# The softmax probabilities of the one-map attentions are scaled by VectorE in place of GpSimd

## The chip, the cores and the metric

The kernel runs on one core of a Trainium2 chip. The metric is the device time of one execution in microseconds (us); the median of several executions counts. The engines are named as in the profile: PE is TensorE's matmul and PEld its weight load, DVE is VectorE, ACT is ScalarE, POOL is GpSimd, SP is SyncE, which issues the DMAs.

## The reference, cut to what matters

A sequence of 512 tokens with 1024 features passes two blocks of two layers each, all in float32. Three of the attentions have one softmax map per head:

- attention A, in both layers of the first block: 8 heads of 64, causal, keys selected by an index score;
- MLA attention, in both layers of the second block: 4 heads, queries and keys of 96, all 512 keys;
- cross attention, in both layers of the second block: 4 heads of 64 on 256 memory rows.

```python
def one_block(qblk):
    sc = jnp.einsum('bqhd,bkhd->bhqk', qblk, k).astype(jnp.float32) * scale
    p = jax.nn.softmax(sc, axis=-1)
    return jnp.einsum('bhqk,bkhe->bqhe', p.astype(v.dtype), v)
```

A fourth, attention B of the first block, subtracts two softmax maps (`a1 - lam * a2`). The change does not touch it.

## The kernel before, in words

All engine programs are written out by hand, with semaphores between engines, and each stage ends in a barrier of all engines. Weights stream in as tiles of 128x1024: SyncE loads a tile into `raw` (a ring of 2, `Weights.load`, L341), ScalarE copies its rounded high part (`split_high`, L350), GpSimd subtracts it for the low part (`split_low`, L359), and TensorE makes three passes per product with high and low parts (`product`, L373 to L375). `split_low` of a tile waits for the tile's high part.

`attention_work` (L674) writes the four engine programs of an attention. Its unit `n` is one block of 128 queries of one head; units go in pairs over two heads, so the query block `i` is `(n % 8) // 2`. `width(i)` is the number of keys: 128, 256, 384, 512 in the causal attention A, always 512 in MLA attention, 256 in cross attention. For a unit:

- TensorE computes the scores into a bank (`scores`, L698);
- VectorE takes the row maximum: L793 with the selection bias in attention A, L796 in the others, which then negate and scale it (L799 in MLA attention, L801 in cross attention);
- ScalarE takes the exponential with its row sum (L760);
- VectorE takes the reciprocal of the sum (L809), one step later;
- GpSimd multiplies the exponentials by it into `prob(n)` (L834), one of 2 buffers in attention A and one of 4 in the others (`depth`); it waits for the reciprocal, and for the transposes of unit `n - depth`;
- TensorE transposes the block (`turn`, L707), `lag` steps after the scores (2 in attention A, 4 in the others);
- ScalarE copies the transposed block to `PT` (L769);
- TensorE multiplies by the values after each 8 units (`value`, L713), and ScalarE copies the result out (L778).

TensorE takes two units at a time: scores, scores, turn, turn. Other work of the stage is laid between the steps by `side_pe`, `side_act`, `side_dve` and `side_pool`. In attention A these are seven tiles of gate products, half a tile per pair of units (`gate_half`), each followed by a multiplication on VectorE that empties the bank (`gate_scale`, L1209; the next gate product waits for it), the splits of their weight tiles, and the normalization of attention B's output at the start. In MLA attention it is the preparation of the memory in eight chunks: ScalarE's scaled copy and square (L503, L509), VectorE's low part and sum (L513, L520), one chunk per step. In cross attention there is none. There GpSimd's program is all splits up to the attention, then the attention, then all splits behind it.

For a map count of 2 (attention B) GpSimd scales the second map (L829) and VectorE combines both (L817); that stays.

Of the kernel before, what the change touches and what calls it, by code (L numbers as in the profile page):

```python
# [18 lines left out]
ALU = mybir.AluOpType  # L19
# [552 lines left out]
def build(nc, x_in, w1, small1, const_in, p_in, w2, small2, masks_in, mem_in, pos_in, out):  # L572
    sem = Semaphores(nc)

    def sb(name, shape, dt=F32):
        return nc.alloc_sbuf_tensor(name, shape, dt)
# [14 lines left out]
    tmp = sb("tmp", [P, 10, SEQ])  # L591
# [11 lines left out]
    stat = sb("stat", [P, 4, 32])  # L603
# [70 lines left out]
    def attention_work(heads, maps, scale, q, k, width, bias, v, m_out, out_of, n_blocks, causal, neg_lambda=None, side_act=None, side_dve=None,  # L674
# [3 lines left out]
        E, LOGIT = 0, 4  # L678
        lag, PROB = (2, (8, 9)) if bias else (4, (4, 5, 6, 7))
        depth = len(PROB)  # L680

        def prob(n):

            return tmp[:, PROB[n % depth], 0:width(unit(n)[1])]

        def unit(n):

            two, r = divmod(n, 2 * NT)
            return 2 * two + r % 2, r // 2
# [92 lines left out]
        def run_dve(dve):  # L782
            for step in range(N + 1):
                if step < N:
                    n = step
                    h, i = unit(n)
                    for m in range(maps):
                        s = n * maps + m
                        dve.wait_ge(sem("scored"), s + 1)
                        if bias:  # L790
                            if s >= 4:
                                dve.wait_ge(sem("exp_done"), s - 3)
                            dve.tensor_tensor_reduce(tmp[:, LOGIT + s % 4, 0:width(i)], banks[s % 4][:, 0:width(i)], bias(i),  # L793
                                                     1.0, -2 * MASKED, ALU.add, ALU.min, stat[:, 0, s:s + 1]).then_inc(sem("max_ready"), 1)
                            continue
                        dve.tensor_reduce(stat[:, 0, s:s + 1], banks[s % 4][:, 0:width(i)], AX.X, ALU.max).then_inc(sem("max_ready"), 1)  # L796
                        dve.wait_ge(sem("max_ready"), s + 1)
                        if query_col:
                            dve.tensor_scalar(stat[:, 1, s:s + 1], stat[:, 0, s:s + 1], query_col(h, i), -1.0, ALU.mult, ALU.mult).then_inc(sem("neg_ready"), 1)  # L799
                        else:  # L800
                            dve.tensor_scalar(stat[:, 1, s:s + 1], stat[:, 0, s:s + 1], -scale, None, ALU.mult).then_inc(sem("neg_ready"), 1)  # L801
                if side_dve:
                    side_dve(dve, step, "scores")
                n = step - 1
                if 0 <= n:
                    h, i = unit(n)
                    s = n * maps
                    dve.wait_ge(sem("exp_done"), s + maps)
                    dve.reciprocal(stat[:, 3, s:s + maps], stat[:, 2, s:s + maps]).then_inc(sem("rsum_ready"), 1)  # L809
                    if maps == 2:  # L810
                        dve.wait_ge(sem("rsum_ready"), n + 1)
                        dve.tensor_scalar(stat[:, 3, s + 1:s + 2], stat[:, 3, s + 1:s + 2], neg_lambda, None,
                                          ALU.mult).then_inc(sem("lambda_ready"), 1)
                        dve.wait_ge(sem("second_scaled"), n + 1)
                        if n >= depth:
                            dve.wait_ge(sem("transposed"), n - depth + 1)
                        dve.scalar_tensor_tensor(prob(n), tmp[:, E + s % 4, 0:width(i)], stat[:, 3, s:s + 1],  # L817
                                                 tmp[:, E + (s + 1) % 4, 0:width(i)], ALU.mult, ALU.add).then_inc(sem("prob_ready"), 1)
                if side_dve:
                    side_dve(dve, step, "end")  # L820

        def run_pool(pool):
            for n in range(N):
                h, i = unit(n)
                s = n * maps
                if maps == 2:
                    e2 = tmp[:, E + (s + 1) % 4, 0:width(i)]
                    pool.wait_ge(sem("lambda_ready"), n + 1)
                    pool.tensor_scalar(e2, e2, stat[:, 3, s + 1:s + 2], 1.0, ALU.mult, ALU.mult).then_inc(sem("second_scaled"), 1)  # L829
                else:  # L830
                    pool.wait_ge(sem("rsum_ready"), n + 1)
                    if n >= depth:
                        pool.wait_ge(sem("transposed"), n - depth + 1)
                    pool.tensor_scalar(prob(n), tmp[:, E + s % 4, 0:width(i)], stat[:, 3, s:s + 1], 1.0,  # L834
                                       ALU.mult, ALU.mult).then_inc(sem("prob_ready"), 1)
                if side_pool:
                    side_pool(pool, n)
        return run_pe, run_act, run_dve, run_pool

    def attention(weights, prefetch, work, before=None):  # L840
# [1845 lines left out]
```

## Time and profile before

| | |
|---|---|
| median of 3 runs | 3483.81 us (3483.07 to 3484.43) |
| profiled execution | 3483.18 us |
| its span | 3481.4 us |
| PE busy | 3182.5 us (91%) |
| DVE busy | 1670.7 us (48%) |
| ACT busy | 1435.2 us (41%) |
| POOL busy | 1576.3 us (45%) |
| POOL, L359 (low parts) | 482 of 2430 ns |
| POOL, L834 (probabilities) | 128 of 562 ns |
| attention A, first layer | 294.6 to 384 us of the span |
| MLA attention, first layer | 2072.8 to 2121.9 us |
| cross attention, first layer | 2229.7 to 2254 us |
| PE busy in attention A, first layer | 80.25 of 89.4 us |

The shares of busy time are averages over stages that differ. For a change inside three of them the stages have to be read apart. Each attention stands twice in the program, once per layer.

### The profile page before, as it was taken

How to read it: one execution, taken by the hardware profiler on the slowest of the kernel's cores; microseconds unless marked ns; L12 is line 12 of the kernel's file. 1: busy time of each engine (PE TensorE's matmuls, PEld its weight loads, DVE VectorE, ACT ScalarE, POOL GpSimd, SP SyncE). 2: the span in 40 equal slices, each digit the busy share in tenths (PEclk: the TensorE clock that was granted, in tenths of full speed). 3: DMA queues.
4: the chain of work that ended last, by engine and by line, in shares of the span. 5: the costliest groups of instructions: out<-in, count | busy, mean ns of one | idle time of the engine just before them, and what ended most of it. 6: DMA issues, size and time to landing. Idle time of an engine off the chain costs nothing. (4 is left out here: it accounts for less than half of the span.)

```text
span 3481.4 us, 39157 instructions
## 1 busy us (share of the span) xinstructions
PE 3182.5 (91%) x14620; PEld 2474.4 (71%) x14620; DVE 1670.7 (48%) x2524; ACT 1435.2 (41%) x2281; POOL 1576.3 (45%) x870
## 2 busy tenths in 40 slices
PE   7978899999998799999999967899999985979999
PEld 6655688878766567887878735578887852758877
DVE  2773347731357533775235883433313785443320
ACT  4736533333384554333343454432223355352221
POOL 4623545544563354554456332334445432234443
PEclk8989999999899999999999978999999997989999
DMA  3111233323211112332322101223333200213333
GB/s 112 61 55 43 69 95 97 97 91 103 76 61 61 37 55 91 103 97 94 103 86 89 52 12 37 66 81 97 96 103 98 67 25 27 65 49 97 97 97 103
DMA packets 73740, 265.09 MB, mean 76 GB/s; under 512 B 8656, under 2 KB 9168, under 8 KB 73168
## 3 DMA queue, kind: packets, MB, share of 16 engines
q1 hardware_dynamic: 73552, 262.59, 24.1%
q8 instruction: 117, 1.92, 0.2%
q14 instruction: 71, 0.58, 0.1%
HBM read 260.46 MB, written 2.10 MB: 75 GB/s over the span
## 5 line engine op out<-in xcount | busy, mean ns | idle before, releaser
L359 POOL TENSOR_TENSOR low<-raw,high 128x1024 fp32r<-128x1024 f32 x482 | 1170.7, 2430 | 1298.8 <-ACT high L350 1276.0
L374 PE MATMUL bank<-slot_r,low 128*128 128x512 f32 (+2 forms) x3636 | 1434.6, 395 | 0.0
L375 PE MATMUL bank<-slot_r,high 128*128 128x512 f32 (+2 forms) x3636 | 1432.1, 394 | 0.0
L373 PE MATMUL bank<-slot_r,high 128*128 128x512 f32 (+1 forms) x3316 | 1339.9, 404 | 100.0 <-POOL low L359 22.5
L350 ACT ACTIVATE high<-raw 128x1024 fp32r<-128x1024 f32 x482 | 507.3, 1054 | 848.2 <-PE bank L375 819.1
L373 PEld LDWEIGHTS bank<-slot_r,high 128*128 128x128 f32 x3316 | 636.5, 192 | 286.5 <-issue 69.4
L374 PEld LDWEIGHTS bank<-slot_r,low 128*128 128x128 f32 (+1 forms) x3636 | 696.4, 192 | 148.9 <-issue 9.2
L375 PEld LDWEIGHTS bank<-slot_r,high 128*128 128x128 f32 (+1 forms) x3636 | 695.4, 191 | 149.8
L1568 DVE SCALAR_TENSOR_TENSOR tmp<-padded,small,tmp 128x512 f32<-128x512 f32 x176 | 209.9, 1251 | 0.0
L834 POOL TENSOR_SCALAR tmp<-tmp,stat 128x512 f32<-128x512 f32 (+3 forms) x128 | 72.0, 562 | 195.4 <-DVE stat L809 167.1
L698 PE MATMUL bank<-slots 64*128 64x256 f32 (+4 forms) x384 | 96.1, 509 | 44.5 <-PEq L320 40.7
L503 ACT ACTIVATE slot_r<-slots,small 128x512 fp32r<-128x512 f32 (+1 forms) x80 | 54.7, 684 | 196.6 <-DVE slots L1547 61.1
L2615 DVE TENSOR_TENSOR tmp<-bank,rs 128x512 f32<-128x512 f32 x44 | 30.4, 692 | 207.3 <-PE bank L375 196.3
L707 PE MATMUL bank<-const,tmp 128*128 128x128 f32 x432 | 74.8, 292 | 59.9 <-ACT PT L769 25.9
L1559 DVE TENSOR_TENSOR padded<-bank,rs 128x512 f32<-128x512 f32 x88 | 60.4, 686 | 138.7 <-PE bank L375 126.5
L2048 DVE SCALAR_TENSOR_TENSOR slots<-padded,small,slots 128x512 f32<-128x512 f32 x128 | 122.0, 1009 | 0.0
L707 PEld LDWEIGHTS bank<-const,tmp 128*128 128x128 f32 x432 | 52.6, 147 | 91.8 <-issue 39.4
L2509 ACT ACTIVATE tmp<-tmp 128x512 f32<-128x512 f32 x44 | 27.8, 633 | 211.6 <-DVE tmp L2615 211.6
L769 ACT ACTIVATE PT<-bank 128x256 f32<-128x256 f32 (+3 forms) x160 | 72.1, 456 | 98.8 <-PE bank L713 51.9
L2625 DVE TENSOR_TENSOR tmp<-bank,rs 128x512 f32<-128x512 f32 x16 | 11.1, 691 | 210.8 <-PE bank L375 210.8
L760 ACT ACTIVATE tmp<-tmp,stat 128x128 f32<-128x128 f32 (+3 forms) x128 | 71.0, 555 | 97.6 <-DVE stat L793 97.0
L1576 DVE TENSOR_TENSOR slots<-slots,bank 128x512 f32<-128x512 f32 x16 | 11.0, 687 | 197.0 <-PE bank L375 197.0
(310 smaller groups left out, 3661.6 us busy)
## 6 DMA issues: line engine op xcount, KB each, us to landing
raw<-w SPq DMA_DIRECT2D x482, 512.0 KB, 3.5
slots<-x_in SPq DMA_DIRECT2D x4, 512.0 KB, 6.6
slots<-mem_in SPq DMA_DIRECT2D x2, 1024.0 KB, 4.9
out<-slots SPq DMA_DIRECT2D x8, 256.0 KB, 4.8
const<-const_in SPq DMA_DIRECT2D x1, 1073.5 KB, 10.6
padded<-p_in SPq DMA_DIRECT2D x2, 512.0 KB, 5.5
tmp<-masks_in SPq DMA_DIRECT2D x1, 512.0 KB, 11.4
small<-small SPq DMA_DIRECT2D x2, 231.5 KB, 2.7
```

The costliest lines, as they stand in the source:

```text
L350: act.activation(self.high[:, t % PARTS, :], self.raw[:, t % RING, :], ACT.Copy).then_inc(self.sem("tile_high"), 1)
L359: pool.tensor_tensor(self.low[:, t % PARTS, :], self.raw[:, t % RING, :], self.high[:, t % PARTS, :].bitcast(F32), ALU.subtract).then_inc( ...
L373: pe.matmul(acc, lhs[0], rhs[1], start=first, stop=False)
L374: pe.matmul(acc, lhs[1], rhs[0], start=False, stop=False)
L375: return pe.matmul(acc, lhs[0], rhs[0], start=False, stop=last)
L698: pe.matmul(banks[s % 4][:, 0:width(i)], q(h, m, i), k(h, m, width(i)), start=True, stop=True).then_inc(sem("scored"), 1)
L707: mm = pe.transpose(banks[4 + n % 2][:, j * P:j * P + P], prob(n)[:, j * P:j * P + P], cst("ident"))
L760: act.activation(tmp[:, E + s % 4, 0:width(i)], src, ACT.Exp, scale=by, bias=most, accum_out=stat[:, 2, s:s + 1]).then_inc(sem("exp_done"), 1)
L769: act.activation(PT[:, h % 2, 0:b, i * P:i * P + P], banks[4 + n % 2][:, 0:width(i)].rearrange("p (b t) -> p b t", b=b), ACT.Copy).then_in ...
L834: pool.tensor_scalar(prob(n), tmp[:, E + s % 4, 0:width(i)], stat[:, 3, s:s + 1], 1.0, ALU.mult, ALU.mult).then_inc(sem("prob_ready"), 1)
L1568: dve.scalar_tensor_tensor(o, padded_t[:, s % 4, 15 - tap:15 - tap + SEQ], s1("conv_w", (2 - tap) * 2 * FC + ch), o, ALU.mult, ALU.add).th ...
L2048: ins = dve.scalar_tensor_tensor(o, src, s2(w, 2 * j + c), o, ALU.mult, ALU.add)
```

## The change

The branch for one map moves from GpSimd's program to the end of VectorE's step. VectorE waits for its own reciprocal and for the buffer, multiplies, and signals `prob_ready`. Nothing else is altered. Lines behind the added ones are shifted: in the changed kernel the new multiplication is L823, and the gate multiplication L1209 is L1208.

```diff
@@ run_dve, after the reciprocal of unit n
                         dve.scalar_tensor_tensor(prob(n), tmp[:, E + s % 4, 0:width(i)], stat[:, 3, s:s + 1],
                                                  tmp[:, E + (s + 1) % 4, 0:width(i)], ALU.mult, ALU.add).then_inc(sem("prob_ready"), 1)
+                    else:
+                        dve.wait_ge(sem("rsum_ready"), n + 1)
+                        if n >= depth:
+                            dve.wait_ge(sem("transposed"), n - depth + 1)
+                        dve.tensor_scalar(prob(n), tmp[:, E + s % 4, 0:width(i)], stat[:, 3, s:s + 1], None, ALU.mult).then_inc(sem("prob_ready"), 1)
                 if side_dve:
                     side_dve(dve, step, "end")
@@ run_pool
                     pool.wait_ge(sem("lambda_ready"), n + 1)
                     pool.tensor_scalar(e2, e2, stat[:, 3, s + 1:s + 2], 1.0, ALU.mult, ALU.mult).then_inc(sem("second_scaled"), 1)
-                else:
-                    pool.wait_ge(sem("rsum_ready"), n + 1)
-                    if n >= depth:
-                        pool.wait_ge(sem("transposed"), n - depth + 1)
-                    pool.tensor_scalar(prob(n), tmp[:, E + s % 4, 0:width(i)], stat[:, 3, s:s + 1], 1.0,
-                                       ALU.mult, ALU.mult).then_inc(sem("prob_ready"), 1)
                 if side_pool:
                     side_pool(pool, n)
```

GpSimd's queue in attention A, first layer, from unit 14 to unit 31, before (L834 is a probability, L359 a low part):

```order
L834 TENSOR_SCALAR tmp<-tmp,stat 128x512 x2
L359 TENSOR_TENSOR low<-raw,high 128x1024
L834 TENSOR_SCALAR tmp<-tmp,stat 128x128 x2
L834 TENSOR_SCALAR tmp<-tmp,stat 128x256 x2
L359 TENSOR_TENSOR low<-raw,high 128x1024
L834 TENSOR_SCALAR tmp<-tmp,stat 128x384 x2
L834 TENSOR_SCALAR tmp<-tmp,stat 128x512 x2
L359 TENSOR_TENSOR low<-raw,high 128x1024
```

The same queue in the changed kernel, for the whole stage (L1303 is a low part of attention B's output):

```order
L1303 TENSOR_TENSOR slot_r<-slots,slot_r 128x512
L359 TENSOR_TENSOR low<-raw,high 128x1024 x2
L1303 TENSOR_TENSOR slot_r<-slots,slot_r 128x512 x2
L359 TENSOR_TENSOR low<-raw,high 128x1024
L1303 TENSOR_TENSOR slot_r<-slots,slot_r 128x512
L359 TENSOR_TENSOR low<-raw,high 128x1024 x5
```

The probabilities that stood between two low parts are gone, and with them their waits.

VectorE's queue in MLA attention, first layer, one step with memory work and the next step's first rows, before:

```order
L809 RECIPROCAL stat<-stat 128x1
L796 TENSOR_REDUCE stat<-bank 128x1
L799 TENSOR_SCALAR stat<-stat,col 128x1
L513 SCALAR_TENSOR_TENSOR slot_r<-slots,small,slot_r 128x256
L520 TENSOR_TENSOR slots<-slots 128x256
L809 RECIPROCAL stat<-stat 128x1
```

And in the changed kernel:

```order
L809 RECIPROCAL stat<-stat 128x1
L823 TENSOR_SCALAR tmp<-tmp,stat 128x512
L796 TENSOR_REDUCE stat<-bank 128x1
L799 TENSOR_SCALAR stat<-stat,col 128x1
L513 SCALAR_TENSOR_TENSOR slot_r<-slots,small,slot_r 128x256
L520 TENSOR_TENSOR slots<-slots 128x256
L809 RECIPROCAL stat<-stat 128x1
```

The multiplication stands between a reciprocal and the next unit's reduction.

VectorE's queue in attention A, first layer, around the gate multiplication of units 15 to 17, before and, behind it, in the changed kernel:

```order
L793 ISA tmp,stat<-bank,selbias 128x128
L793 ISA stat 128x1
L809 RECIPROCAL stat<-stat 128x1
L1209 TENSOR_TENSOR slots<-bank,rs 128x512
```

```order
L793 ISA tmp,stat<-bank,selbias 128x128
L793 ISA stat 128x1
L809 RECIPROCAL stat<-stat 128x1
L823 TENSOR_SCALAR tmp<-tmp,stat 128x128
L1208 TENSOR_TENSOR slots<-bank,rs 128x512
```

The probability of the unit before now stands ahead of the gate's multiplication.

## Rows read from the trace of the kernel before

**Rows 1.** Line L834: durations (min/median/max), and who waited for it (us, times)
```profile
L834 POOL TENSOR_SCALAR tmp<-tmp,stat x128: 372/536/704, 296.3 to 3079.5; 128x256 f32<-128x256 f32 x48, 128x512 f32<-128x512 f32 x48, 128x128 f32<-128x128 f32 x16, 128x384 f32<-128x384 f32 x16
...
  PEld bank L707: 28.6, 26
  PE bank L707: 8.0, 6
```

**Rows 2.** Timeline, MLA attention, one step: start us, us, engine, line, operation, idle before
```profile
2086.01 0.78 ACT L760 ACTIVATE tmp<-bank,stat,col 128x512 f32<-128x512 f32 x1
2087.95 0.79 ACT L760 ACTIVATE tmp<-bank,stat,col 128x512 f32<-128x512 f32 x1
...
2086.59 0.15 DVE L809 RECIPROCAL stat<-stat 128x1 f32<-128x1 f32 x1
2086.66 0.67 DVE L796 TENSOR_REDUCE stat<-bank 128x1 f32<-128x512 f32 x1
2087.80 0.48 DVE L513 SCALAR_TENSOR_TENSOR slot_r<-slots,small,slot_r 128x256 fp32r<-128x256 f32 x1 [0.22 <-ACT slot_r L503]
2088.54 0.15 DVE L809 RECIPROCAL stat<-stat 128x1 f32<-128x1 f32 x1
```

**Rows 3.** Timeline, cross attention: first and last of 12 exponentials, one reduction and negation
```profile
2231.18 0.47 ACT L760 ACTIVATE tmp<-bank,stat 128x256 f32<-128x256 f32 x1 [0.19 <-DVE stat L801]
2239.42 0.48 ACT L760 ACTIVATE tmp<-bank,stat 128x256 f32<-128x256 f32 x1
...
2235.20 0.41 DVE L796 TENSOR_REDUCE stat<-bank 128x1 f32<-128x256 f32 x1
2235.64 0.15 DVE L801 TENSOR_SCALAR stat<-stat 128x1 f32<-128x1 f32 x1
```

**Rows 4.** One line, L1146: duration ns min/median/max of its forms
```profile
L1146 DVE TENSOR_SCALAR selbias<-PT,slots x6: 354/421/488, 86.5 to 1016.6; 128x256 f32<-128x256 f32 x2, 128x384 f32<-128x384 f32 x2, 128x512 f32<-128x512 f32 x2
```

**Rows 5.** Timeline, VectorE: a reciprocal and the operation that waits for it
```profile
2960.68 0.18 DVE L2535 RECIPROCAL col<-col 128x4 f32<-128x4 f32 x1 [18.80 <-ACT col L2454]
2960.89 0.29 DVE L2540 TENSOR_SCALAR tmp<-const,col 128x128 f32<-128x128 f32 x1
```

**Rows 6.** Timeline, attention A, first layer: around two gate multiplications
```profile
349.07 1.05 ACT L350 ACTIVATE high<-raw 128x1024 fp32r<-128x1024 f32 x1
350.64 0.16 DVE L809 RECIPROCAL stat<-stat 128x1 f32<-128x1 f32 x1 [0.89 <-ACT tmp L760]
351.35 2.37 POOL L359 TENSOR_TENSOR low<-raw,high 128x1024 fp32r<-128x1024 f32 x1
351.95 0.60 PE L707 MATMUL bank<-const,tmp 128*128 128x128 f32 x4
352.24 0.67 DVE L1209 TENSOR_TENSOR slots<-bank,rs 128x512 f32<-128x512 f32 x1
353.54 0.50 PE L373 MATMUL bank<-slot_r,high 128*128 128x512 f32 x1
...
357.31 1.05 ACT L350 ACTIVATE high<-raw 128x1024 fp32r<-128x1024 f32 x1
359.09 0.16 DVE L809 RECIPROCAL stat<-stat 128x1 f32<-128x1 f32 x1 [1.13 <-ACT tmp L760]
362.04 0.50 PE L373 MATMUL bank<-slot_r,high 128*128 128x512 f32 x1
```

**Rows 7.** Timeline: a low part on GpSimd and two VectorE operations beside it
```profile
2984.46 2.40 POOL L359 TENSOR_TENSOR low<-raw,high 128x1024 fp32r<-128x1024 f32 x1 [7.15 <-ACT high L350]
2984.61 2.52 DVE L2540 TENSOR_SCALAR tmp<-const,col 128x128 f32<-128x128 f32 x2
```

**Rows 8.** Busy time by stretch, MLA attention: value products, and what came before the second
```profile
2098.06:2101.64 3.58, 3.58 (x17) 1.06 (x16) 0.16 (x1) 0.06 (x1) 3.02 (x2) 1.00 0.00 0
2113.05:2119.60 6.55, 6.52 (x16) 1.71 (x16) 0.00 (x0) 0.00 (x0) 0.00 (x0) 0.56 0.00 0
2102.00:2108.60 6.60, 3.32 (x16) 1.72 (x14) 2.04 (x6) 6.55 (x13) 2.41 (x3) 1.00 0.26 79
```

## Prediction

> **What bounds the kernel now.** The change touches 128 multiplications, so I first looked at who waits for them. On GpSimd they take 372 to 704 ns, and TensorE waited for one of them 8.0 us in all and its weight loads 28.6 us [rows 1]. Next I took apart the six stages that hold them, attention A, MLA attention and cross attention, each for two layers. Each stands between barriers or in one engine order, so that what a stage loses the program loses. They have different limits. Attention A is TensorE's once its gate products run: it goes from transposes (351.95) through the next scores to the next gate product (353.54) without a stop [rows 6]. In MLA attention TensorE is light and ScalarE sets the pace: one step is an exponential, its sum, a copy, and a scaled copy and a square of the memory, from 2086.01 to 2087.95 in the same order each time; the exponential to exponential distance is 1.95 us, and VectorE's is the same, reciprocal to reciprocal [rows 2]. What the reader is to see there is VectorE's idle time inside the step: 0.22 us. It is the second engine of that loop, with nearly no room. Cross attention is alike without the memory work: 12 exponentials start from 2231.18 to 2239.42 [rows 3].
>
> **The change part by part.** It removes 128 multiplications from GpSimd and puts one behind each reciprocal on VectorE, with two waits ahead of it (for the reciprocal, and for the transposes that free the buffer).
>
> *Price of one.* The nearest row is L1146: the same operation with one per-row scalar, SBUF to SBUF, 354, 421 and 488 ns for 256, 384 and 512 columns [rows 4]. I take these. The bounds: below, 0.29 us, which L2540 takes for 128 columns [rows 5]; above, the GpSimd times of [rows 1] (0.70 for 512). An operation that reads a reciprocal starts 0.21 us after it (2960.68 to 2960.89) [rows 5], and one that doesn't wait starts some 0.08 before the recorded end of the one ahead: the reciprocal at 2086.59 lasts 0.15, and the reduction starts at 2086.66 [rows 2]. A 512-column scale so holds VectorE 0.41 and a 256-column one 0.28, plus 0.13 of waiting (0.20 from the reciprocal where it was 0.07, [rows 2]): 0.54 and 0.41 us per step. [...]
>
> *MLA attention, per layer.* VectorE's step is 1.95 - 0.22 = 1.73 us of work [rows 2]; with 0.54 it is 2.27, over ScalarE's 1.95. Eight steps carry memory work (the eight chunks), each loses 0.32: 2.6 us until the first value products can start. Behind them the tail is ScalarE's and TensorE's and keeps its length: VectorE has two reductions and four reciprocals left in it and is idle for the most part. Two layers: **+5.2**. Bounds: a scale of 0.29 us makes the step 2.07 and the term +2, one of 0.70 makes it 2.48 and the term +8.5.
>
> *Cross attention, per layer.* Reduction to negation is 0.44 (2235.20 to 2235.64) [rows 3], negation to reciprocal 0.07, reciprocal to scale 0.20, scale 0.28: 0.99 us per step. From the first exponential to the twelfth there are eleven steps; the first has no scale (0.52), ten at 0.99, and 0.2 until the first ends: 10.6 against 8.24 now, +2.4. The products behind wait for the copy after the twelfth. Two layers: **+4.8**; bounds +2 and +8.
>
> *Attention A, per layer.* Here TensorE needs a probability one or two steps later, behind half a tile of gate products, so its own length costs nothing. What costs is GpSimd's other work. The split of a weight tile's low part (L359, 2.37 us) stood behind a probability on GpSimd's queue; now it starts when its high part is done (349.07 + 1.05, so 350.2 in place of 351.35) [rows 6]. The scale on VectorE reads and writes SBUF only, and such an operation does not run beside L359: of two L2540 that started at 2984.61, 0.15 after an L359, both ended only at 2987.13, where the clean ones take 0.29; the L359 ran from 2984.46 to 2986.86 [rows 5, 7]. So the scale of unit 19, due at 350.64 + 0.20 = 350.84, ends at about 352.75. Its transposes were due on TensorE at 352.2: +0.65. Then VectorE still owes the maximum (0.49), the reciprocal, the scale of unit 20 (0.20 + 0.35) and only then the gate's multiplication L1209 (0.67), which the next gate product waits for: 354.6 against 353.54, **+1.07** [rows 6]. Three places per layer look so (L1209 at 333.5, 352.2, 371.5). At the other two (341.4, 360.6) the split runs from 358.45 to 360.8, the 512-column scale due at 359.3 ends at 361.0, and 0.22 + 0.20 + 0.21 + 0.69 + 0.1 later the gate product may start, at 362.4 against 362.04 [rows 6]: +0.4. The last transposes lose 0.2. Sum 3.2 + 0.8 + 0.2 = 4.2, two layers **+8.4**. The stage's first 28 us belong to ScalarE's table loads; there the shorter hand-over gains some tenths and collisions lose some: I take zero, bounds -1 and +1 per layer. The bounds of the term: +0.5 if nothing collides, +11.
>
> *GpSimd itself* is freed of 72 us; nobody waits for its splits in these stages, so this is worth nothing. In cross attention the next tile's split now runs before the attention instead of behind it, and the tile is used after it either way. DMA issues are the same and come earlier.
>
> **Sum:** 8.4 + 5.2 + 4.8 = +18.4 us. The profiled execution took 3483.18 us, 0.6 below the median of the runs, 3483.81; on the median that is 3502.2, and I write 3502.0. A measurement of this kernel tells 0.2% (7 us) from no change.
>
> **The rivals.**
> *No collision.* If the scale gets past L359, attention A loses 0.2 per layer and the sum is 5.2 + 4.8 + 0.4 = 10.4: 3494. For it: only [rows 7] speaks against, and with another first input. 0.16. [...]
>
> *The clock falls.* [...] Against: no row shows a fall during the steps themselves. 0.12.
>
> *The cover holds.* If VectorE's waits in both loops hide most of the scale (the 0.22 of [rows 2] is what this one step shows; early steps and the tail have more), some 3 us are left: 3487. 0.08.
>
> *The shorter chain wins*, slower turned to faster. One hand-over and 0.1 to 0.2 us of duration per probability go: a 512-column one is ready 0.25 us sooner after its reciprocal (0.70 + 0.10 against 0.49 + 0.05). Where TensorE waits for it, 32 times [rows 1], this gives 32 x 0.2 = 6.4 us, and an L359 ending sooner in front of a VectorE operation with two SBUF inputs gives 1 us twice: 3475. It decides if VectorE's loop in MLA has more than 0.54 us of room per step; the row shows 0.22. [...] 0.05.
>
> **How the numbers follow.** The forecast has 0.59. Range 3489 to 3511: it holds the forecast with its bounds, the no-collision case and nearly all of the clock case, and leaves out the last two and the far bounds. Slower by over 0.2% is the forecast, no collision and the clock: 0.87. Within 0.2%: 0.08. Faster: 0.05.
>
> **What would show it.** In MLA attention VectorE's reciprocals 2.2 to 2.3 us apart where they were 1.95, with no idle time left, and ScalarE's exponentials waiting for the negation; the stage 2.6 us longer. In cross attention exponentials 1 us apart and the stage 2.4 longer. In attention A an L359 starting right behind L350, a scale of 1.5 to 2.4 us beside it, TensorE's transposes waiting for VectorE, and the stage 4 us longer. Wrong would be: all scales at 0.3 to 0.5 us beside L359 (no collision); a granted clock of 0.5 in the first value products; or an idle time on VectorE that outlasts the scale.

## Result and profile after

The changed kernel takes 3501.51 us (median of 5 runs, 3500.14 to 3504.93), against 3483.07 for the kernel before in the same measurement: 1.0054 times as long, 95% interval 1.0043 to 1.0065. That is +18.4 us; the prediction was 3502.0. The profiled execution of the change is the slowest of its five, 3504.93 us with a span of 3503.2.

The page after, busy time of each engine, and the line of the multiplication (L823, in place of [rows 1]):

```profile
PE 3196.1 (91%) x14620; PEld 2479.2 (71%) x14620; DVE 1740.9 (50%) x2652; ACT 1439.4 (41%) x2281; POOL 1507.1 (43%) x742
...
L823 DVE TENSOR_SCALAR tmp<-tmp,stat x128: 285/421/1905, 297.6 to 3100.6; 128x256 f32<-128x256 f32 x48, 128x512 f32<-128x512 f32 x48, 128x128 f32<-128x128 f32 x16, 128x384 f32<-128x384 f32 x16
...
  PEld bank L707: 56.1, 54
  PE bank L707: 13.1, 19
```

The median multiplication became shorter (421 ns against 536), the longest one far longer (1905 against 704), and TensorE waits for it 69.2 us in place of 36.6.

**MLA attention** after, timeline of VectorE, one step of the first layer (answers [rows 2]):

```profile
2102.32 0.16 DVE L809 RECIPROCAL stat<-stat 128x1 f32<-128x1 f32 x1
2102.51 0.49 DVE L823 TENSOR_SCALAR tmp<-tmp,stat 128x512 f32<-128x512 f32 x1
2102.91 0.68 DVE L796 TENSOR_REDUCE stat<-bank 128x1 f32<-128x512 f32 x1
2103.63 0.21 DVE L799 TENSOR_SCALAR stat<-stat,col 128x1 f32<-128x1 f32 x1
2103.76 0.48 DVE L513 SCALAR_TENSOR_TENSOR slot_r<-slots,small,slot_r 128x256 fp32r<-128x256 f32 x1
2104.15 0.42 DVE L520 TENSOR_TENSOR slots<-slots 128x256 f32<-128x256 f32 x1
2104.49 0.16 DVE L809 RECIPROCAL stat<-stat 128x1 f32<-128x1 f32 x1
```

No idle time is left, and the step is 2.17 us (1.95 before).

**Attention A** after, timeline of the first layer around a gate multiplication (answers [rows 6]):

```profile
353.19 2.40 POOL L359 TENSOR_TENSOR low<-raw,high 128x1024 fp32r<-128x1024 f32 x1 [9.05 <-ACT high L350]
353.63 0.17 DVE L809 RECIPROCAL stat<-stat 128x1 f32<-128x1 f32 x1 [0.89 <-ACT tmp L760]
353.83 1.91 DVE L823 TENSOR_SCALAR tmp<-tmp,stat 128x256 f32<-128x256 f32 x1
...
355.80 0.44 PE L707 MATMUL bank<-const,tmp 128*128 128x128 f32 x2 [0.44 <-DVE tmp L823]
356.66 0.68 DVE L1208 TENSOR_TENSOR slots<-bank,rs 128x512 f32<-128x512 f32 x1
```

The low part starts right behind its high part (352.06 + 1.05), and a multiplication of 256 columns that begins 0.64 us later lasts 1.91, until the low part is over; alone the same multiplication takes 0.35. Six per layer do this (1.82 to 1.91 us). Two multiplications per layer of MLA attention do it too (1.54 and 1.72 us, behind the steps with memory work). They cost nothing there: the second value products start 15.0 us after the first, as in before.

**Where the time went.** One row is a kernel, one column a stretch, in us: how much more lies between the starts of the same two TensorE instructions than in the profile of before. The last four rows are experiments of the next section.

| | start to 41 | A, layer 1 (294 to 400) | A, layer 2 (1192 to 1300) | other stretches to 2072 | from 2072 to the end | sum |
|---|---|---|---|---|---|---|
| the change | +1.4 | +6.5 | +6.4 | +0.6 | +6.9 | +21.8 |
| A only | -0.8 | +5.1 | +6.5 | +4.4 | +0.2 | +15.4 |
| A only, from the bank | -0.4 | -0.2 | -0.1 | -0.5 | 0.0 | -1.1 |
| A only, short low parts | -0.7 | -0.3 | +1.0 | +2.9 | +2.4 | +5.3 |
| the same again | -0.5 | +0.9 | +1.0 | +5.4 | +2.3 | +9.2 |

The first column lies ahead of every changed instruction and has either sign; it is not the change's. So does the time up to 294 us, with 1.8 of the 4.4 us of A only in the fourth column. The profiles of the change and of A only are the slowest executions of their five, 3.4 and 3.0 us over the median, so their rows add up to more than the medians say.

### The profile page after: what moved, and what is told of

It is laid out like the page before. It is cut to its first block and busy times, and to the rows that moved or that the text cites. A ratio compares the mean times of both kernels' runs of the same rounds, so it can differ in the third digit from the quotient of the medians.

```text
span 3503.2 us, 39157 instructions
## 1 busy us (share of the span) xinstructions
PE 3196.1 (91%) x14620; PEld 2479.2 (71%) x14620; DVE 1740.9 (50%) x2652; ACT 1439.4 (41%) x2281; POOL 1507.1 (43%) x742
## 5 line engine op out<-in xcount | busy, mean ns | idle before, releaser
L359 POOL TENSOR_TENSOR low<-raw,high 128x1024 fp32r<-128x1024 f32 x482 | 1171.9, 2433 | 1509.6 <-ACT high L350 1479.9
L707 PE MATMUL bank<-const,tmp 128*128 128x128 f32 x432 | 84.0, 314 | 65.9 <-ACT PT L769 26.3
L698 PEld LDWEIGHTS bank<-slots 64*128 64x128 f32 (+1 forms) x384 | 42.1, 210 | 86.2 <-issue 80.7
```

The source lines that it names most:

```text
L359: pool.tensor_tensor(self.low[:, t % PARTS, :], self.raw[:, t % RING, :], self.high[:, t % PARTS, :].bitcast(F32), ALU.subtract).then_inc( ...
L698: pe.matmul(banks[s % 4][:, 0:width(i)], q(h, m, i), k(h, m, width(i)), start=True, stop=True).then_inc(sem("scored"), 1)
L707: mm = pe.transpose(banks[4 + n % 2][:, j * P:j * P + P], prob(n)[:, j * P:j * P + P], cst("ident"))
```

## The experiments

All are times of whole kernels beside runs of before, which has a median of 3483.0 to 3483.3 in each measurement.

### One stage at a time

The place of the multiplication becomes a choice of each caller (`on_dve`); each run has one stage on VectorE and the others on GpSimd.

```diff
-                    else:
+                    elif on_dve(n):
                         dve.wait_ge(sem("rsum_ready"), n + 1)
@@ run_pool
+                elif not on_dve(n):
+                    pool.wait_ge(sem("rsum_ready"), n + 1)
...
```

> Only attention A scales on VectorE; MLA and cross attention stay as before. By the traces of before and after, each layer of A lost 4.8 us and TensorE's lower clock behind it 1.6 to 1.9 more: the theory expects +12.5 to +13.5 us (about 3496.5), and a stage of 94.2 us where before has 89.3. My recorded terms alone (+8.4 for A) give 3492. If the stages were not independent and the shares came from MLA or cross attention, this run is near +5. The +1.4 us that the profiled run of the change lost in its first 41 us, ahead of every changed instruction, should be missing here or come and go between runs.

> Only MLA attention scales on VectorE. [...] Sum near 0: -1 to +1 us in all. [...] Rival (VectorE's room hides the scale): exponentials stay 1.95 apart.

> Only cross attention scales on VectorE. Recorded term +4.8 (exponentials 0.99 apart where they were 0.72 to 0.75); by the trace of the change +3.6 per layer, +7.2 in all, because TensorE's transposes and value products there also run at the lower clock. If only the VectorE loop counts: +4.8; with the clock: +7.

Measured: attention A 3495.59 us (+12.6, ratio 1.0035, 1.0022 to 1.0047), MLA attention 3483.56 (+0.6; 1.0000, 0.9991 to 1.0009), cross attention 3490.25 (+7.3; 1.0019, 1.0010 to 1.0027). The sum is +20.4 against +18.4 for all at once. So attention A holds nearly two thirds, cross attention nearly all the rest, and MLA attention nothing that these runs can tell. In cross attention the clock may have a part. Busy time by stretch (us, then PE, PEld, DVE, ACT, POOL busy, PEclk, DMA share, GB/s), before and then cross attention on VectorE:

```profile
2234.50:2241.50 7.00, 5.78 (x32) 2.86 (x34) 5.20 (x25) 5.92 (x24) 3.85 (x8) 1.00 0.00 1
```

```profile
2235.00:2242.00 7.00, 6.24 (x22) 3.13 (x22) 5.96 (x27) 5.05 (x19) 0.00 (x0) 0.52 0.00 1
```

In seven microseconds TensorE gets through 22 matmuls in place of 32, at a granted clock of 0.52 in place of 1.00. VectorE's own step is 0.98 us, where I had worked out 0.99, but two of its steps are longer (1.52 and 1.22 us), since it waits for scores. Its timeline at the first of them:

```profile
2237.18 0.15 DVE L810 RECIPROCAL stat<-stat 128x1 f32<-128x1 f32 x1
2237.37 0.35 DVE L826 TENSOR_SCALAR tmp<-tmp,stat 128x256 f32<-128x256 f32 x1
2237.64 0.42 DVE L797 TENSOR_REDUCE stat<-bank 128x1 f32<-128x256 f32 x1
2238.09 0.15 DVE L802 TENSOR_SCALAR stat<-stat 128x1 f32<-128x1 f32 x1
2238.16 0.15 DVE L810 RECIPROCAL stat<-stat 128x1 f32<-128x1 f32 x1
...
2239.14 0.42 DVE L797 TENSOR_REDUCE stat<-bank 128x1 f32<-128x256 f32 x1 [0.44 <-PE bank L699]
```

The kernel before has two such waits as well, and longer ones (0.56 against 0.44 us), at a granted clock of 1.00:

```profile
2236.58 0.42 DVE L796 TENSOR_REDUCE stat<-bank 128x1 f32<-128x256 f32 x1 [0.56 <-PE bank L698]
...
2240.01 0.42 DVE L796 TENSOR_REDUCE stat<-bank 128x1 f32<-128x256 f32 x1 [0.56 <-PE bank L698]
```

So the waits are not new, and VectorE's slower steps have used up only a part of them. Whether at a granted clock of 1.00 they would have used up all, no run shows: in both layers of the three profiles with this multiplication on VectorE (the change, cross attention alone, and the change with attention A read from the bank) the clock is 0.56 to 0.71 over the twelve exponentials, where before has 1.00. It can be low without it too. With MLA attention alone on VectorE, the first layer's cross attention, which is before's, ran at 0.50 from 2233 to 2239 us and its stage lost 1.8 us.

### Attention A without the collision, by another source

The exponentials are written into the bank of the scores and the multiplication reads them there. All queues keep the order of the change.

```diff
+        from_bank = bias and maps == 1
+        def weighed(s, i):
+            return (banks[s % 4] if from_bank else tmp[:, E + s % 4, :])[:, 0:width(i)]
...
-                        pe.wait_ge(sem("max_ready" if bias else "exp_done"), s - 3)
+                        pe.wait_ge(sem("prob_ready" if from_bank else "max_ready" if bias else "exp_done"), s - 3)
...
-                        act.activation(tmp[:, E + s % 4, 0:width(i)], src, ACT.Exp, scale=by, bias=most,
+                        act.activation(weighed(s, i), src, ACT.Exp, scale=by, bias=most,
...
-                        dve.tensor_scalar(prob(n), tmp[:, E + s % 4, 0:width(i)], stat[:, 3, s:s + 1], None, ALU.mult)
+                        dve.tensor_scalar(prob(n), weighed(s, i), stat[:, 3, s:s + 1], None, ALU.mult)
```

> Attention A alone scales on VectorE, but its exponentials are written into the bank of the scores, and the multiplication reads them there, so that its only tensor in SBUF is the output. Collision theory: a multiplication that reads PSUM does not need what GpSimd's L359 holds, so it takes 0.35 to 0.7 us wherever an L359 runs, no one lasts over 1 us, and the term falls from about +13 to between -2 and +2 us. Rival (the cost is the multiplication's place in VectorE's queue ahead of the gate multiplication, not the collision): with 0.1 to 0.2 us more per multiplication it stays at +13 or grows. A third way: any VectorE operation that writes SBUF waits beside L359, then some still last 1.5 us or more and the term stays.

Measured: 3483.12 us (1.0000, 0.9991 to 1.0009). Its line, durations in ns, who waited, and one multiplication beside a low part:

```profile
L830 DVE TENSOR_SCALAR tmp<-bank,stat x64: 349/551/754, 295.7 to 1273.8; 128x128 f32<-128x128 f32 x16, 128x256 f32<-128x256 f32 x16, 128x384 f32<-128x384 f32 x16, 128x512 f32<-128x512 f32 x16
...
  PEld bank L712: 9.9, 7
  PE bank L712: 8.0, 6
...
355.64 2.41 POOL L359 TENSOR_TENSOR low<-raw,high 128x1024 fp32r<-128x1024 f32 x1 [6.09 <-ACT high L350]
356.50 0.75 DVE L830 TENSOR_SCALAR tmp<-bank,stat 128x512 f32<-128x512 f32 x1
```

The median multiplication is longer than the change's in attention A (551 against 421 ns), none lasts over 0.75 us beside a low part, and the 12.6 us are gone. So it is not the write to SBUF by itself that makes it long; with the input in PSUM the operation passes. Beside a low part the traces show 1.91 us from SBUF and 0.75 at most from PSUM; what in the hardware makes this difference, none shows. The rival *no collision* would have had the multiplication pass from SBUF too.

### Attention A without the collision, by shorter low parts

```diff
-            pool.tensor_tensor(self.low[:, t % PARTS, :], self.raw[:, t % RING, :], self.high[:, t % PARTS, :].bitcast(F32),
+            c = slice(0, cols)
+            pool.tensor_tensor(self.low[:, t % PARTS, c], self.raw[:, t % RING, c], self.high[:, t % PARTS, c].bitcast(F32),
...
-                weights.split_low(pool, base + min((n - first_gate) // 4 + 3, n_gates + 2))
+                weights.split_low(pool, base + min((n - first_gate) // 4 + 3, n_gates + 2), 64)
```

> As the run with attention A alone on VectorE (multiplication from SBUF to SBUF), but the low parts that GpSimd makes inside attention A cover only 64 of a tile's 1024 columns; the other 960 keep what an earlier tile left there. So the order of all queues stays, and only GpSimd's busy time goes. Collision theory: every multiplication lasts 0.28 to 0.5 us, and attention A's first layer takes 87 to 88 us, as with the multiplication that reads PSUM (87.5), where A alone on VectorE took 92.9. Rival (order of the queue): 92 us still.

> The kernel before (all multiplications on GpSimd) with the same 64-column low parts inside attention A as in the run before this one with short low parts; the other 960 columns keep an earlier tile's. It tells whether the 10 us that the short low parts left in the median come from leaving them out (other data, another rhythm of TensorE) or from VectorE's multiplications. If they belong to leaving out: about 3493 with a spread of over 10 us here too. If they belong to VectorE's place in the queue: 3482 to 3484.

> The kernel with short low parts and attention A on VectorE once more, beside its counterpart on the same chip. Attention A's first layer to its last product about 2 us shorter than before's, as in the first profile. The time follows the mean granted clock: 3482 at 0.952, 3493 at 0.947, 3496 at 0.945, as in its first ten runs; median again 3490 to 3495.

> Attention A alone on VectorE, with both: short low parts of GpSimd (64 of 1024 columns, the rest an earlier tile's) and the multiplication that reads the scores' bank. No collision is possible in either way. It tells what the 10 us of the two runs with short low parts and a multiplication from SBUF are. If short low parts under VectorE's multiplications cost time by themselves (TensorE's rhythm in attention A, and its clock in later stages): 3490 or more here too. If they hang on the multiplication from SBUF: 3482 to 3484, as with the bank alone.

Measured: VectorE from SBUF with short low parts 3492.99 us (1.0024, 1.0015 to 1.0033) and again 3494.45 (1.0030, 1.0018 to 1.0041); GpSimd with short low parts 3483.52 (1.0001); VectorE from the bank with short low parts 3482.92 (1.0000). This is a miss of the run's time. What the stage shows is nearly as the theory has it: no multiplication lasts over 0.86 us (I had written 0.5; the 0.86 stands beside a low part of attention B's output, which was not shortened), and from the first gate products to the stage's end (330 to 381) the stage loses 1.0 and 1.1 us, where the change loses 4.9, the bank 1.6 with full and with short low parts, and GpSimd with short low parts 0.0. So leaving out most of a low part gains nothing by itself, 3.9 of the 4.9 us are the collision, and 1.0 is the multiplication's place ahead of the gate's. The whole stage of the first layer was 1.9 us shorter than before's in the first profile and 1.0 us longer in the second, where I had expected 2 us shorter again; the difference lies ahead of 330 us, where TensorE's granted clock was 1.00 in the first (from 320 to 328) and 0.63 in the second. And most of the run's time did not come back; it lies in stages that no edit touches (the last two columns of the table ahead of the sum), where TensorE's granted clock is lower, for one 0.50 in place of 0.71. Behind the same idle time of 6.8 us, the same stretch of the same code, in before and with short low parts:

```profile
1333.90:1339.60 5.70, 5.51 (x18) 4.44 (x19) 0.13 (x1) 0.35 (x1) 2.36 (x1) 0.71 0.34 119
```

```profile
1333.30:1339.00 5.70, 5.45 (x13) 4.31 (x14) 0.19 (x1) 0.42 (x1) 2.36 (x1) 0.50 0.37 132
```

TensorE gets through 13 matmuls in place of 18. Both profiles with short low parts show it at the same places, though one enters this stretch at -0.5 us and the other at +3.3. The executions of one kernel scatter with the clock too: of those with short low parts the shortest, 3481.96 us and so level with before, had a mean granted clock of 0.952, the longest, 3496.3, one of 0.945. Why this kernel's mean granted clock (median 0.947 and 0.946 in the two measurements) is below that of its three neighbours (0.951 from the bank with full and with short low parts, 0.950 for GpSimd with short low parts) stays open. It also limits the claim on attention A: the collision is shown as the cause of 3.9 us of each layer's stage, not as the cause of each of the 12.6 us.

### The price of a step in MLA attention

Twice: each multiplication of MLA attention is made a second time, behind the first. Sum moved: GpSimd adds the squares of the memory.

```diff
+                            dve.tensor_scalar(prob(n), tmp[:, E + s % 4, 0:width(i)], stat[:, 3, s:s + 1], None, ALU.mult).then_inc(sem("prob_once"), 1)
+                            dve.wait_ge(sem("prob_once"), n + 1)
@@ the other kernel, side_dve and side_pool of MLA attention
-                if step >= 4:
-                    memory.add(dve, step - 3)
+            if 3 < n < 3 + KC:
+                memory.add(pool, n - 3)
```

> Only MLA attention on VectorE, and each multiplication is made twice, the second behind the first's end. If VectorE bounds the step, the second adds its 0.49 plus 0.04 until it may start: reciprocals 2.70 us apart in the steps with memory work where they were 2.17, 8 x 0.53 = 4.2 us more per layer, 3492 in all. If VectorE had room left: less than 0.3 us per step and 3486 to 3488.

> Only MLA attention on VectorE, and the sum of the memory's squares (0.39 us per step on VectorE) is made by GpSimd, which does nothing there. VectorE's step falls from 2.17 to 1.83 us, ScalarE's 1.95 bounds again, and the 1.8 us per layer come back: 3480. If GpSimd's sum collides with the multiplication or with the low part (two inputs in SBUF), steps stay at 2.1 to 2.3 and the time at 3483 to 3485, with multiplications of 0.7 us and over.

Measured: twice 3500.11 us (1.0049, 1.0035 to 1.0063), sum moved 3482.80 (1.0000, 0.9991 to 1.0009). The reciprocals are 2.69 us apart when made twice, as worked out: VectorE sets this loop, and 0.52 us more per step is paid in full. The time was 8 us more than I wrote: the steps without memory work are bound by VectorE then too (first value products 5.5 us later than with one multiplication, not 4.2). That makes 11 of the 17 us in two layers. The rest lies behind them, where the clock took time: in the second layer, for one, the first 16 value products took 5.35 us at a granted clock of 0.69 where before has 3.65 at 1.00. With the sum on GpSimd the step did not get shorter but longer, 2.30 us. VectorE and GpSimd there:

```profile
2091.86 0.96 DVE L513 SCALAR_TENSOR_TENSOR slot_r<-slots,small,slot_r 128x256 fp32r<-128x256 f32 x1
...
2091.82 0.72 POOL L520 TENSOR_TENSOR slots<-slots 128x256 f32<-128x256 f32 x1 [1.60 <-ACT slots L509]
```

L513, with two inputs in SBUF, now lasts 0.96 us beside the sum, against 0.48 without it: the same collision, on another operation. Still the run is no longer than before. Its first value products start 2.7 us later than before's, but TensorE's second ones, which start 15.0 us after the first here as in before, ran at a granted clock of 1.00 here. These second value products, after the change and with the sum on GpSimd (before: [rows 8]):

```profile
2129.60:2135.50 5.90, 5.71 (x16) 1.52 (x16) 0.00 (x0) 0.09 (x1) 0.00 (x0) 0.64 0.00 0
```

```profile
2115.90:2119.70 3.80, 3.65 (x16) 1.07 (x16) 0.00 (x0) 0.05 (x1) 0.00 (x0) 1.00 0.00 0
```

16 products took 6.52 us before, 5.71 after the change and 3.65 here, at granted clocks of 0.56, 0.64 and 1.00. What VectorE lost ahead of them, the clock gave back.

### Together

> What the runs so far suggest as best: attention A on VectorE with the exponentials in the scores' bank, MLA attention on GpSimd for units 0 to 9 and on VectorE for 10 to 15 (no memory work in those steps), cross attention on GpSimd. Attention A's stages 1.8 and 1.7 us shorter; behind them TensorE's clock gives 1.6 back if it falls there as in the run with PSUM; MLA attention's stages 0.5 to 1 shorter each. Sum -1 to -5.5: 3480 (3478 to 3482.5), below what 5 rounds tell surely from before.

> All 128 multiplications on VectorE as in the change, but attention A's read the scores' bank. If the three stages add up and the collision with L359 is what attention A lost: 0 (A) + 0.6 (MLA) + 7.2 (cross) = 3491 (3489 to 3493). If attention A's loss came from something that the stages do to each other, it stays near 3500.

Measured: the mixture 3483.97 us (1.0002, 0.9993 to 1.0011), no better than before; I had written 3480. The change with attention A read from the bank: 3491.01 (1.0022, 1.0013 to 1.0031), as the sum of the single stages has it, 10.5 us better than the change and 8 worse than before. No version here beats the kernel before.

## Why the prediction was right

The total came out to within 0.5 us, but two of its three terms were too small and the third too large: attention A 12.6 us (alone, the median) against 8.4, cross attention 7.3 against 4.8, MLA attention 0.6 against 5.2. Alone the three add up to 20.4, and 2 us of that are within what these runs can't tell. The sign holds, and so do the collision in attention A and VectorE's longer steps in the other two; what TensorE's clock made of them was not foreseen. That the total agrees this well is luck.

- **Attention A, inside the stage: right.** The multiplication beside L359 was to cost 1.07 us at three places, 0.4 at two and 0.2 at the end. Measured as steps of the offset: 1.27, 0.92 and 0.92, then 0.42 and 0.46, and 0.93 at the end, 4.9 in place of 4.2. The mis-sized one is the last: the last multiplication before the value products collides in full (1.82 us). The row that the collision was read from, [rows 7], is two operations in one: the first L2540 lasted 2.32 us, to 2986.93, and only then the second began and took its 0.27. The prediction has both held to the end; only the first was, and its sum does not change by that.
- **Attention A, behind the stage: missed.** TensorE's next products run at a lower granted clock, 0.66 in place of 1.00. The first 5 us behind the stage, before and after:

```profile
385.50:390.50 5.00, 5.00 (x22) 4.16 (x23) 4.11 (x3) 4.97 (x8) 4.47 (x3) 1.00 0.35 105
```

```profile
391.80:396.80 5.00, 5.00 (x15) 3.96 (x16) 4.09 (x3) 4.97 (x8) 4.54 (x3) 0.66 0.34 105
```

  1.6 us per layer, in both layers. The sum took the clock as unchanged outside the stretches of [rows 8]. These 1.6 us also turn up without a long collision: in 9 of the 22 such stages of attention A in the other eleven experiments, some of them with before's own attention A. Each of these 9 had gained 1.5 to 3.4 us against before between 294 and 330 us (or the same place of the second layer). There before's clock falls (0.57 from 320 to 328) and the bank's does not (1.00). In the four stages with long collisions, of the change and of A only, the 1.6 us came every time and a gain there, of 1.35 us, only once. That speaks for counting them to the change's cost; how the collision would bring them about is not shown.
- **MLA attention: too large.** The step is 2.17 us and not 2.27. I had given the negation its recorded 0.21 us, while the next operation starts 0.13 after it. The first value products came 1.8 us late, not 2.6. "Behind them the tail keeps its length" was the step that failed: the second value products were 0.8 us shorter (5.71 for 6.52, granted clock 0.64 for 0.56) and the first products of the next stage caught up more (the first 32 took 5.40 us for 6.99, granted clock 0.75 for 0.52 over the stage's first 6 us), so that the stage and what follows it up to cross attention lost nothing (-0.1 and -0.4 us).
- **Cross attention: the step right (0.98 for 0.99 us), the stage not.** 12 exponentials took 11.30 us where I had 10.6, since I had counted no wait for scores, though before has two, and both stayed, if shorter. The stage lost 3.6 us per layer after the change and 2.9 alone, not 2.4: 3.1 up to the first value products in both, and the rest of the 3.6 behind them, where TensorE works through the same products more slowly (granted clock 0.72 for 1.00 between the first and the second value products of the first layer).
- **The rivals.** *No collision* is out: it would have left attention A near 0. *The clock falls* came true, but in cross attention (0.56 over the exponentials of the change, 1.00 in before) and behind attention A (0.66 for 1.00), and not in the first value products of MLA attention (1.00 in both layers of the change); only with the multiplication made twice did it fall there, in one layer of two (0.69). The upper end of the range, 3511, allowed for a fall there in each layer; the one that a run shows cost 1.7 us (5.35 for 3.65). In MLA attention's second value products the clock gave time back (0.64 for 0.56). *The cover holds* and *The shorter chain wins* are out as to the sum; the shorter hand-over is real (421 against 536 ns) and without the collision it about pays for the multiplication's place in the queue: attention A from the bank is at 0.

## What to carry to other kernels

Before an elementwise operation moves from GpSimd to VectorE, look at what GpSimd will do at that time: here the freed queue let a 2.4 us operation start earlier, and short VectorE operations behind the reciprocal then lasted until its end (1.82 to 1.91 us). If the operation must be on VectorE, take its input from PSUM where a bank is free: it is slower by itself (0.75 against 0.49 us for 512 columns) and was worth 10 us. A collision has its price only where somebody waits for the operation: the two per layer in MLA attention (1.54 and 1.72 us) cost nothing. And price a loop by the distance of the starts in the trace, not by recorded durations, then check which clock TensorE is granted behind it: in this kernel it raised the loss of one stage by a third (4.9 to 6.5 us in attention A) and cancelled that of another (1.8 us in MLA attention).

## What was not expected of the hardware

- A VectorE multiplication with one input in SBUF and one per-row scalar lasted up to 1.91 us beside a GpSimd operation with two inputs (L359), against 0.35 alone for the same 256 columns; with the input in PSUM and the output in SBUF it lasted 0.75 us at most beside it.
- TensorE's granted clock differs at places that hardly differ: over the first 5 us behind attention A and an idle time of some 2.3 us it was 1.00 in before and 0.66 in the kernel from the bank and in the kernel with the memory's sum moved, whose attention A is before's, instruction for instruction.
- Executions of one kernel differ by up to 14 us with the mean granted clock, 0.952 to 0.945.
